# A hybrid encoder block on one core: squares of x summed from PSUM, state tables loaded in pieces, and gate scaling moved

## What is computed

```python
hn = rms_norm(h, norm1_g[l])
q, k, v, u, g_na, g_ssm = jnp.split(hn @ w_in[l], IN_SPLITS, axis=-1)
y_na = neighbourhood_attention(q, k, v, na_rpb[l]).reshape(b, L, NA_WIDTH) @ w_proj_na[l]
y_ssm = s5_branch(u, ssm_lam_re[l], ..., ssm_d[l], w_glu[l]) @ w_proj_ssm[l]
mixed = jax.nn.sigmoid(g_na) * y_na + jax.nn.sigmoid(g_ssm) * y_ssm
h = h + mixed @ w_out[l]
h = h + conv_gated_ffn(rms_norm(h, norm2_g[l]), w_up[l], conv_w[l], conv_b[l], w_down[l])
h = rms_norm(h, final_g)
```

## Time and profile before

| what | value |
|---|---|
| three runs | 1461.24, 1463.76, 1464.51 us; median 1463.76 |
| profiled execution | 1463.71 us, its span 1462.0 us |
| TensorE matmul busy | 1441.5 us, 99% of the span |
| VectorE, ScalarE, GpSimd busy | 603.3, 663.3, 1013.9 us |
| TensorE idle, 0 to 40 / 40 to 80 / 80 to 120 us | 2.7 / 6.0 / 0.4 us |
| TensorE idle, 560 to 1462 us | 7.6 us, nearly all behind its last product |

### The profile page before, as it was taken

One profiled execution on the slowest core, in us unless ns is written; L12 is line 12 of the kernel. 1 busy time (PEld: TensorE's weight loads), 2 busy tenths in 40 slices (PEclk: granted clock), 3 DMA queues, 4 the chain that ended last, 5 costly groups with the idle time before them and its releaser, 6 DMA issues.

```text
span 1462.0 us, 30268 instructions
## 1 busy us (share of the span) xinstructions
PE 1441.5 (99%) x11735; PEld 1373.0 (94%) x11735; DVE 603.3 (41%) x1147; ACT 663.3 (45%) x897; POOL 1013.9 (69%) x475
## 2 busy tenths in 40 slices
PE   9899999999999999999999999999999999999997
PEld 9899999998998999999999999999999998888886
DVE  7758888887545255543322222222222221003002
ACT  7346544432453554454544444444444443334333
POOL 5000058840678688898888888888888887888885
PEclk9999999999999999999999999999999999999999
DMA  8895456655665455665565655555555556555553
GB/s 290 237 222 182 136 173 203 185 155 144 189 195 181 134 174 183 231 213 178 176 191 181 186 183 178 184 186 177 183 186 182 179 185 201 187 187 178 196 187 130
DMA packets 238305, 271.50 MB, mean 186 GB/s; under 512 B 21904, under 2 KB 224016, under 8 KB 237456
## 3 DMA queue, kind: packets, MB, share of 16 engines
q1 hardware_dynamic: 227968, 257.11, 57.0%
q10 hardware_dynamic: 10256, 13.26, 2.8%
HBM read 262.07 MB, written 8.26 MB: 185 GB/s over the span
## 4 chain that ended last, share of the span: by engine, by line
PE 89%; DVE 4%; DMA 2%; issue 2%; ACT 1%; POOL 1%; DVEq 1%; SPq 0%; ACTq 0%; POOLq 0%
PE ps L1468 23%; PE ps L1470 22%; PE ps L1469 22%; PE ps L1789 6%; PE ps L1788 6%; PE ps L1787 6%; PE ps L1625 1%; DMA w_raw<-in_w_in 1%; DVE w_lo L505 1%; POOL w_lo L505 1%; PE ps L1568 1%; DMA x_feature_major<-in_tokens 1%; PE ps L1631 0%; DVE square_ring L956 0%; PE ps L1698 0%
## 5 line engine op out<-in xcount | busy, mean ns | idle before, releaser
L505 POOL TENSOR_TENSOR w_lo<-w_raw,w_hi 128x1024 fp32r<-128x1024 f32 x409 | 985.2, 2416 | 379.5 <-ACT w_hi L501 379.3
L501 ACT ACTIVATE w_hi<-w_raw 128x1024 fp32r<-128x1024 f32 x464 | 489.9, 1060 | 654.4 <-PE ps L1470 456.9
L1468 PE MATMUL ps<-act_hi,w_hi 128*128 128x258 f32 (+2 forms) x2432 | 695.4, 286 | 7.7 <-DVE w_lo L505 6.5
L1470 PE MATMUL ps<-act_hi,w_lo 128*128 128x258 f32 (+2 forms) x2432 | 690.7, 284 | 0.0
L1469 PE MATMUL ps<-act_lo,w_hi 128*128 128x258 f32 (+2 forms) x2432 | 689.2, 283 | 0.0
L1468 PEld LDWEIGHTS ps<-act_hi,w_hi 128*128 128x128 f32 x2432 | 461.2, 190 | 14.3 <-issue 9.9
L1469 PEld LDWEIGHTS ps<-act_lo,w_hi 128*128 128x128 f32 x2432 | 461.8, 190 | 0.1
L1470 PEld LDWEIGHTS ps<-act_hi,w_lo 128*128 128x128 f32 x2432 | 460.3, 189 | 0.0
L1789 PE MATMUL ps<-w_lo,hidden_hi 128*128 128x512 f32 x352 | 140.3, 399 | 0.0
L1788 PE MATMUL ps<-w_hi,hidden_lo 128*128 128x512 f32 x352 | 138.7, 394 | 0.0
L1787 PE MATMUL ps<-w_hi,hidden_hi 128*128 128x512 f32 x352 | 138.3, 393 | 0.0
(11 more groups left out here) (233 smaller groups left out, 1507.5 us busy)
## 6 DMA issues: line engine op xcount, KB each, us to landing
w_raw<-in_w_up SPq DMA_DIRECT2D x176, 512.0 KB, 3.5
w_raw<-in_w_in SPq DMA_DIRECT2D x128, 512.0 KB, 4.0
w_raw<-in_w_down SPq DMA_DIRECT2D x88, 512.0 KB, 3.5
w_raw<-in_w_out SPq DMA_DIRECT2D x32, 512.0 KB, 3.4
w_raw<-in_w_proj_na SPq DMA_DIRECT2D x16, 512.0 KB, 3.4
w_raw<-in_w_proj_ssm SPq DMA_DIRECT2D x16, 512.0 KB, 3.4
w_raw<-in_w_glu SPq DMA_DIRECT2D x8, 512.0 KB, 3.4
xT<-in_tokens ACTq DMA_DIRECT2D x1, 2176.0 KB, 8.7
```

The lines of the kernel that those rows point to most:

```text
L501: act.activation(slot(whi, k), slot(raw, k), ACT.Copy).then_inc(s_hi, 1)
L505: pool.tensor_tensor(slot(wlo, k), slot(raw, k), slot(whi, k).bitcast(F), ALU.subtract).then_inc(s_lo, 1)
L1468: mm(o, slot(whi, k)[:, cols], xh[:, kt, lo:lo + n], start=kt == 0, stop=False)
L1470: ins = mm(o, slot(wlo, k)[:, cols], xh[:, kt, lo:lo + n], start=False, stop=kt == units * UKT - 1)
```

## The change

- The four quarters' squares go to PSUM banks 4 to 7, one buffer for all, and each square waits for the sum of the quarter before. The first square moves ahead, behind unit 5's high part; the others follow units 7, 8 and 9. The sums read PSUM. `scale_sum` moves from behind unit 9 to behind unit 8, and TensorE waits for all four sums ahead of unit 8.
- GpSimd splits units 6 to 11 instead of 8 to 11.
- The state tables are loaded in four pieces each (two halves of the groups, straight and swapped): b behind the loads of units 18 to 21, c behind those of units 34 to 37, with a semaphore for each. The wait for c is before the first `g_make`.
- VectorE makes low part 13 right behind 12, 16 ahead of the parameter stage that stood before it, and `u_block(3)` behind low part 17, one parameter stage earlier.
- The scaling of `gate_na` moves from behind `gate_block` to behind the row maxima of the same block.

```diff
--- before.py
+++ after.py
@@ -153,7 +153,6 @@
         R2 = at("b_swapped", 87552, [P, DIRS * GROUPS, GROUP])
         pwW1 = at("pow_in", 95744, [P, DIRS * GROUPS, CHUNK])
         pwW2 = at("pow_in_im", 97792, [P, DIRS * GROUPS, CHUNK])
-        xsq = (tr, at("x_squares", o_y + 8704, [P, DEPTH, L]))
         Wn = at("w_nat", 99840, [P, WSLOTS, DIRS, TG, CHUNK * GROUP])
         WT = at("w_tr", 108032, [P, DIRS, PB, P])
         stg = at("qkv_stage", 112128, [P, 2, 2, 2 * WK])
@@ -208,7 +207,7 @@
         s_x = [sem(f"x_loaded_{n}") for n in range(len(X_PARTS))]
         s_gain = sem("gains_loaded")
         s_par = sem("params_loaded")
-        s_tab = sem("state_tables_loaded")
+        s_tab = [sem(f"state_tables_loaded_{n}") for n in "bc"]
         s_fg = sem("final_gain_loaded")
         s_raw = [sem(f"unit_loaded_{i}") for i in range(DEPTH)]
         s_hi = sem("unit_hi_made")
@@ -405,20 +404,24 @@
             sp.dma_start(prm[:, 0:3, :], ssm_params).then_inc(s_par, 16)
             sp.dma_start(dcol[:, :], skip_cols).then_inc(s_par, 16)
             sp.dma_start(cvw[:, :], conv_cols).then_inc(s_par, 16)
-            load_in(U_U, 3 * HALF, 1, range(4))
-
-            def table_load(same, swapped, src):
-                sp.dma_start(same[:, :, :], src).then_inc(s_tab, 16)
-                for h in range(2):
-                    sp.dma_start(swapped[64 * h:64 * h + 64, :, :], src[64 - 64 * h:128 - 64 * h]).then_inc(s_tab, 16)
-
-            load_in(U_U, 3 * HALF, 1, range(4, 6))
+            load_in(U_U, 3 * HALF, 1)
+
+            def table_load(n, piece):
+                same, swapped, src = ((R1, R2, b_rows), (C1, C2, c_rows))[n]
+                gs = slice(GROUPS * (piece % 2), GROUPS * (piece % 2 + 1))
+                if piece < 2:
+                    sp.dma_start(same[:, gs, :], src[:, gs, :]).then_inc(s_tab[n], 16)
+                else:
+                    for h in range(2):
+                        sp.dma_start(swapped[64 * h:64 * h + 64, gs, :], src[64 - 64 * h:128 - 64 * h, gs, :])\
+                          .then_inc(s_tab[n], 16)
+
             sp.wait_ge(s_nl, KT + SEED)
             sp.wait_ge(s_xsq, 4)
-            table_load(R1, R2, b_rows)
-            load_in(U_U, 3 * HALF, 1, range(6, 8))
-            table_load(C1, C2, c_rows)
-            load_in(U_V, 2 * HALF, 0)
+            for k in range(8):
+                load_in(U_V, 2 * HALF, 0, (k,))
+                if 2 <= k < 6:
+                    table_load(0, k - 2)
             for k in range(8):
                 load_in(U_V, 2 * HALF, 1, (k,))
                 if k == 0:
@@ -427,8 +430,10 @@
                 sp.dma_start(U2[64 * g + GROUP * j:64 * g + GROUP * (j + 1), :, :],
                              u_d[:, :, j, :].rearrange("k (b g c) n -> g c (k b) n", b=PB, g=2)[g]).then_inc(s_u2, 16)
 
-            for i in range(ITERS_IN):
-                load_in(U_K, HALF, i)
+            for u in range(16):
+                load_in(U_K, HALF, u // 8, (u % 8,))
+                if 2 <= u < 6:
+                    table_load(1, u - 2)
             for i in range(ITERS_IN):
                 load_in(U_Q, 0, i)
 
@@ -548,8 +553,8 @@
                                        base=(QCOLS - KSTEP) * t + COL_WIN // 2 - 1 - high,
                                        pattern=[[-1, KCOLS - high]], channel_multiplier=1)
                     pool.drain()
-            pool.wait_ge(s_lo, 2 * DEPTH)
-            for k in range(2 * DEPTH, 3 * DEPTH):
+            pool.wait_ge(s_lo, 6)
+            for k in range(6, 3 * DEPTH):
                 lo_unit(pool, 0, k)
 
             pool.wait_ge(s_lo, U_Q + DEPTH - 1)
@@ -614,9 +619,9 @@
                     act.activation(hnh[:, k, :], x0T[:, k, :], ACT.Copy, scale=gains[:, k:k + 1]).then_inc(s_nh, 1)
 
             def x_square(q):
-                if q >= 2:
-                    act.wait_ge(s_xss, q - 1)
-                act.activation(xsq[q % 2][:, :, :], x0T[:, 4 * q:4 * (q + 1), :], ACT.Square).then_inc(s_xsq, 1)
+                if q:
+                    act.wait_ge(s_xss, q)
+                act.activation(ps[:, 4:8, 0:L], x0T[:, 4 * q:4 * (q + 1), :], ACT.Square).then_inc(s_xsq, 1)
 
             hi_unit(act, U_U, 0)
             x_hi(0)
@@ -626,9 +631,13 @@
                 x_hi(q + 1)
                 hi_unit(act, U_U, 2 * q)
                 hi_unit(act, U_U, 2 * q + 1)
-            for q in range(4):
+                if q == 2:
+                    x_square(0)
+            for q in range(1, 4):
                 x_square(q)
-                hi_unit(act, U_U, 8 + q)
+                hi_unit(act, U_U, 7 + q)
+            hi_unit(act, U_U, 11)
+            norm_root(0, L)
 
             def u_store(n):
                 act.wait_ge(s_u, n + 1)
@@ -637,7 +646,6 @@
 
             v = lambda n: prm[:, n, :]
             hi_unit(act, U_U, 12)
-            norm_root(0, L)
             hi_unit(act, U_U, 13)
             u_store(0)
             act.wait_ge(s_par, 48)
@@ -946,20 +954,23 @@
             for k in range(4):
                 x_lo(k)
             lo(1)
+            def x_sum(q):
+                dve.wait_ge(s_xsq, q + 1)
+                tile = dve.reduce_sum(sq[:, min(q, 1), :], ps[:, 4:8, 0:L].rearrange("p k t -> p t k"), AX.X)
+                if q:
+                    dve.drain()
+                    tile = dve.tensor_tensor(sq[:, 0, :], sq[:, 0, :], sq[:, 1, :], ALU.add)
+                tile.then_inc(s_xss, 1)
+                dve.drain()
+
             for q in range(1, 4):
                 for k in range(4 * q, 4 * (q + 1)):
                     x_lo(k)
-                lo(2 * q)
-                lo(2 * q + 1)
+                if q < 3:
+                    lo(2 * q)
+                    lo(2 * q + 1)
             for q in range(4):
-                dve.wait_ge(s_xsq, q + 1)
-                dve.reduce_sum(sq[:, min(q, 1), :], xsq[q % 2][:, :, :].rearrange("p k t -> p t k"), AX.X)
-                dve.drain()
-                if q:
-                    dve.tensor_tensor(sq[:, 0, :], sq[:, 0, :], sq[:, 1, :], ALU.add).then_inc(s_xss, 1)
-                    dve.drain()
-                else:
-                    dve.nop().then_inc(s_xss, 1)
+                x_sum(q)
 
             def gate_block(gate, f, two_banks):
                 dve.tensor_tensor(gate[:, f:f + 2, :], two_banks,
@@ -1029,6 +1040,7 @@
             dve.wait_ge(s_par, 48)
             dve.wait_ge(s_lo, 3 * DEPTH)
             lo(12)
+            lo(13)
             dve.wait_ge(s_pa, 1)
             mul(v(4), v(0), v(3))
             mul(v(5), v(1), v(3))
@@ -1041,7 +1053,6 @@
                 dve.scalar_tensor_tensor(out=v(5), in0=v(10), scalar=-c, in1=v(5), op0=ALU.mult, op1=ALU.add)
             dve.drain()
             dve.tensor_scalar(v(7), v(5), PI_BELOW, -PI_BELOW, ALU.min, ALU.max).then_inc(s_pcp, 1)
-            lo(13)
             u_block(2)
             lo(14)
             lo(15)
@@ -1050,6 +1061,7 @@
             dve.tensor_copy(tsp[0:NB, 2:4], ps[0:NB, 7, 2:4])
             dve.tensor_scalar(qsc[:, 0:2], ps[:, 7, 4:6], SCALE, None, ALU.mult)
             dve.tensor_scalar(qsc[0:2, 2:3], ps[0:2, 7, 6:7], SCALE, None, ALU.mult).then_inc(s_tsp, 1)
+            lo(16)
             dve.wait_ge(s_pa, 3)
             mul(v(10), v(9), v(9))
             dve.drain()
@@ -1059,10 +1071,11 @@
             mul(a1[1], v(6), v(8))
             dve.drain()
             cmul(a2, a1, a1, tmp)
-            lo(16)
+            lo(17)
+            u_block(3)
             cmul((pw[:, 3, 0, :], pw[:, 3, 1, :]), a2, a1, tmp)
             cmul((pw[:, 4, 0, :], pw[:, 4, 1, :]), a2, a2, tmp)
-            lo(17)
+            lo(18)
             dve.tensor_scalar(v(15), a1[0], 1.0, None, ALU.subtract)
             mul(v(16), v(0), v(0))
             mul(v(17), v(1), v(1))
@@ -1077,8 +1090,6 @@
             dve.tensor_tensor(v(18), v(18), v(19), ALU.add)
             dve.tensor_tensor(v(20), v(20), v(21), ALU.subtract)
             dve.drain()
-            lo(18)
-            u_block(3)
             lo(19)
             mul(gq[:, 0, 0, :], v(18), v(16))
             mul(gq[:, 0, 1, :], v(20), v(16))
@@ -1134,7 +1145,7 @@
 
             for n in range(22, 32):
                 lo(n)
-            dve.wait_ge(s_tab, 96)
+            dve.wait_ge(s_tab[0], 96)
             w_make(0)
             lo(32)
             lo(33)
@@ -1164,6 +1175,7 @@
                 if t + WSLOTS < KH:
                     w_make(t + WSLOTS)
                 elif t == KH - 2:
+                    dve.wait_ge(s_tab[1], 96)
                     g_make(0)
 
 
@@ -1277,6 +1289,10 @@
                 att_scores(b)
                 if b == 0:
                     meta_probs()
+                if b >= G_ATT - G_SCAN:
+                    n = b - (G_ATT - G_SCAN)
+                    dve.tensor_tensor(gate_na[:, 2 * n:2 * n + 2, :], gate_na[:, 2 * n:2 * n + 2, :],
```

(13 more changed lines are left out.)

## The result

The changed kernel takes 1466.58 us, median of 18 runs (1463.80 to 1470.38); beside it the kernel before took 1461.91 us, median of 18 (1459.38 to 1465.27). The ratio is 1.0032, 95% interval 1.0025 to 1.0040: slower by some 4.7 us, where the forecast was 0.7 us less, too little to be told from no change. The measured time lies in the stated range of 1459.0 to 1467.0, near its upper end. The profiled execution took 1469.79 us with a span of 1468.1, 6.1 more than before's 1462.0; it is one of the longer ones, so the trace shows the loss somewhat large.

A forecast was written before the change was run, and what follows sets the result against it. TensorE was taken as busy end to end, only its gaps and slow stretches winnable. Front +1.1 us and attention −1.8 give −0.7 on 1463.71: 1463.0 us, range 1459.0 to 1467.0.

The forecast's parts named there:

- The squares: Before unit 8: additions wait for GpSimd instructions, the four sums end at 38.35, unit 8 starts at 38.45, 6.4 us later.
- upper bound of 2.7 us: Top of the range for one quarter's sum from PSUM, 1.3 to 2.7 us, taken as 2.1; called a third above today's.
- the lost race: First square-sum addition issued 0.1 us after GpSimd changes instruction, ends at 30.4; unit 8 2 us later, 1465.0; chance 0.25.
- The clock behind unit 8: After TensorE idles over 6 us before unit 8, slow clock adds 1.75 us; unit 8 ends at 43.3.
- The way back to unit 21: Units 9 to 21: u_block(3) at 65.45, 3.3 us of waiting at units 19 to 21, unit 21 starts at 83.8.
- the front's +1.1: Up to unit 21, start at 83.8 against 82.71: late transfer's 5 us won, unit 8's idle and slow clock paid.
- unit 16 would not wait for its load: With no table ahead, unit 16's load is issued at 50.9, lands in 4.0 us and is used at 65.3.
- Gate scaling: In attention: the three waits on scores, 1.6 us, go with 0.2 for pipeline restarts, −1.8 us; the new place is free.
- The c pieces: Behind units 34 to 37, one piece per unit, v store issued several units' work after the last: likeliest delay 0.
- slower rival: c pieces delay the last v store, VectorE's copies and the k block; 4 us gives 1467; slower cases together 0.14.
- The prediction's own sign of being wrong: Wrong if a gap appears past 120 us, unit 8 starts before 36, or PSUM reduction is under 1 or over 3.

The follow-up runs named there:

- c later: Changed kernel with the four c table pieces behind the loads of units 42 to 45 instead of 34 to 37: 1462.12 us, 0.9994 of the kernel before.
- squares alone: Kernel before with only PSUM squares, GpSimd from unit 6, TensorE's wait before unit 8 and the moved sum over partitions: 1466.41 us, 1.0028.
- gate scaling alone: Kernel before with only the scaling of gate_na moved behind the row maxima: 1463.50 us, 0.9989 of the kernel before.
- tables alone: Kernel before with only the table loads moved, b behind units 18 to 21: c behind 34 to 37 (early) 1463.23 us, 0.9995; behind 42 to 45 1458.20, 0.9969.
- no additions: Changed kernel without VectorE's three additions of square sums; TensorE adds four partial sums in four products with ones: 1461.05 us, 0.9987 of the kernel before.
- PSUM operand: Changed kernel with later quarters' partial sums left in PSUM, so each addition has one SBUF and one PSUM input: 1460.71 us, 0.9981.

## Why the prediction was right and wrong

**The squares: right in mechanism, and in time partly by luck.** The sums were to end at 38.35 and unit 8 to start at 38.45; they ended at 38.47 and it started at 38.52. The reason held too: every addition was held by GpSimd, the last by unit 10, which GpSimd began at 35.82 (35.65 forecast). Two terms were off. The reduction cost 1.29 us where 2.1 was taken, the price of the contiguous elements and not the strided one; it hardly moved the end, since GpSimd's instructions set the pace, as the prediction says. (Its upper bound of 2.7 us is a quarter above today's 2.14 and not a third; nothing hangs on it.) And the chain began 0.76 us late (sum 0 at 23.06 for 22.3), because ScalarE waited for the loads of units 4 and 5. That the end agrees to 0.1 us is luck: in two other executions of the same chain, c later and squares alone, the sums ended at 37.25 and 37.06, and the wait was 4.6 and 4.5 us. What holds in all three is that the third addition is issued 0.35 us behind GpSimd's start on unit 10 and ends 0.2 us behind the end of that unit. The Trainium skill (SBUF — State Buffer, the cacheline note) gives the size of PSUM's lines and says that access that is not contiguous slows matmuls; that a strided read of VectorE gains nothing there was the prediction's conclusion, and it does not hold for this instruction: 1.29 us from PSUM against 2.14 from SBUF for the same elements in the same order. The first addition neither got in at a change of GpSimd's nor missed one by 0.1: its reduction was short, so it was issued 0.8 us behind the change at 26.1 and held to 28.77, between the 28.2 of the forecast and the 30.4 of the lost race.

**The clock behind unit 8: undersized in this execution.** Taken at 1.75 us, as in the earlier trace rows; measured 2.4 (the stretches 39 to 45 and the part of 36 to 39 in which TensorE works). The same place cost 1.4 and 1.7 us behind waits of 4.6 and 4.5 us, with c later and with the squares alone. Behind the 3.4 us at unit 16 of the kernel before, the clock stayed up for another 0.6 us of work; here it is down from the first product on.

**The way back to unit 21: right.** The transposes' results reached VectorE at 60.02 with 1.80 us of idle (1.4 forecast), `u_block(3)` started at 66.26 (65.45 forecast), and the waits at units 19 to 21 are 2.9 us where 3.3 were worked out. Unit 21 at 84.71 against 83.8 is the clock's 0.65 and a little more. So the front's +1.1 was +2.0. Other executions give much the same difference at another level: 82.61 with c later, 80.19 with the front of before in the run of the gate scaling alone. That unit 16 would not wait for its load was right, and that the tables were its cause is shown by the tables alone.

**Gate scaling: right.** 174.6 us of attention became 172.7, −1.9 against −1.8; alone 0.9989. It was cheaper than forecast in its new place: 0.90 us on the mean of six, against 1.73 before.

**The c pieces: the step that failed.** This step was put at nothing in the sum. The prediction had the mechanism as its slower rival, with the store, the copy, VectorE's unbroken chain and the k block, and gave it, with others, a chance of 0.14. The reason given, "they go one piece per unit, and the store is issued several units' work behind the last", does not hold, and SP's rows above show it. One piece per unit is true, but the units' loads do not go out at TensorE's pace: the loads wait for low parts, and VectorE's list gives low parts in pairs with a state matrix between them; so the loads of units 36 and 37 and half of c, 2 MB in all, go out within 3.4 us (118.96 to 122.36), and unit 38 follows at 125.12. The store's last part is issued at 127.15, 4.8 us behind the last piece, which is the work of one and a half units (3.03 us each) and not of several. In the kernel before the DMA share was 0.41 over 120 to 125 and 0.84 over the next 5 us; here it is 0.97 and 1.05 (the stretches above), so the store finds full queues. The rival's price was sized at 1 us per us of delay: 3.7 us of delay gave 3.0 more of waiting, much as said. What was left out is that a wait of 3.4 us takes the clock with it, which the same text had charged at units 8 and 16: 2.9 us more, of which 2.4 reach the scan stage. Together the k stage lost 5.7 where the rival took 4, so its 1467 would have been 1468.7, and the profiled execution is at 1469.8. The prediction's own sign of being wrong, a gap past 120 us, did appear, at 143.41.

**What the sum should have been.** +2.0, +5.7, −1.9 give 5.8 of the 6.1 us of the profiled pair. The runs' medians are 4.7 apart. Neither kernel's front takes the same time in every execution: the kernel before had 3.4 us at unit 16 and the slow clock, the gate-only run 1.45 and a full clock; the changed kernel waited 6.0 us at unit 8, the run with c later 4.6. What of the medians' difference belongs to that, and what to executions in which the store is less late, stays open; the waits were seen in one execution of each kernel only.

## What to carry to other kernels

Before a transfer is moved, list what is issued on every queue in the microseconds behind its new place and what waits for that: here a table first read at 193.8, some 70 us later, went in front of a store wanted at once. An instruction of VectorE with two SBUF inputs beside a busy GpSimd costs up to a whole GpSimd instruction (here up to 2.38 us, where it takes 0.44 alone and GpSimd's takes 2.4); in a serial chain, as here with one buffer, each such addition is paid in full, and an operand in PSUM removes it. And a longer wait of TensorE is to be charged with slow clock besides: in these runs waits of 2.3 to 6.0 us took another 1.4 to 2.9 us, and waits of up to 1.9 us took nothing.

## What the runs showed of the hardware

Summing 4 x 272 elements with the tile index innermost took 2.14 us from SBUF (stride 1088 bytes) and 1.29 from PSUM (a bank's stride), which is the 1.3 estimated for contiguous elements; writing the partial sums to PSUM as well left it at 1.30. The square's ACTIVATE of 1088 elements took 1.06 to 1.08 us into PSUM and 1.09 to 1.12 into SBUF.

TensorE's clock behind its idle times, with what the stretch at 1.2 GHz cost while it worked:

| idle us | where | clock behind it | lost us |
|---|---|---|---|
| 1.45 | unit 16, gate scaling alone | 1.00 | 0 |
| 1.9 | unit 16, squares alone | 1.00 | 0 |
| 2.3 | k block, no additions | 0.50 at once | 2.9 |
| 3.1 | k block, tables alone, c early | 0.50 after 1 us of work | 1.7 |
| 3.4 | unit 16, kernel before | 0.50 after 0.6 us of work | 1.75 |
| 3.4 | k block, PSUM operand | 0.50 at once | 2.4 |
| 3.4 | k block, changed kernel | 0.50 at once | 2.9 |
| 4.5, 4.6 | unit 8, squares alone and c later | 0.50 at once | 1.7, 1.4 |
| 6.0 | unit 8, changed kernel | 0.50 at once | 2.4 |

Within these rows the loss does not grow with the idle time.
